# Layer norms whose sums over the partitions run on four 32-column groups and one folding product, with other products set between them

## Time and profile before

| | us |
|---|---|
| median of 3 runs (lowest, highest) | 2003.59 (2003.43, 2006.44) |
| the profiled execution, its own time | 2002.64 |
| its span, first to last instruction | 2000.9 |
| TensorE busy | 1972.6 (99%) |
| VectorE, ScalarE busy | 752.6 (38%), 401.2 (20%) |
| weights and inputs moved | 510.86 MB, 255 GB/s in the mean |

### The profile page before, as it was taken

How to read it: one execution, slowest core, us unless ns; L and a number is a source line. 1 busy time by engine, 2 the same in 40 slices (tenths; PEclk the granted TensorE clock), 3 DMA queues, 4 the chain that set the end, 5 groups by cost and what they waited for, 6 DMA issues and landing times.

```text
span 2000.9 us, 36477 instructions
## 1 busy us (share of the span) xinstructions
PE 1972.6 (99%) x15686; PEld 1437.2 (72%) x15686; DVE 752.6 (38%) x1766; ACT 401.2 (20%) x945; POOL 0.2 (0%) x4
## 2 busy tenths in 40 slices
PE   9999999999999999999999999999999999999998
PEld 8879999988766656666666666556764578566797
DVE  6847556587521111111111111011317734426725
ACT  1242110114310111000100010000214342223343
POOL 0000000000000000000000000000000000000000
PEclk9999999999999999999999999999999999999999
DMA  9474644455199999999999999999231211122220
GB/s 351 167 279 154 210 169 185 148 210 190 65 416 420 420 420 420 420 420 420 420 420 420 421 421 417 420 420 421 121 105 43 106 43 64 63 103 87 106 85 22
DMA packets 74929, 510.86 MB, mean 255 GB/s; under 512 B 7888, under 2 KB 13200, under 8 KB 13968
## 3 DMA queue, kind: packets, MB, share of 16 engines
q1 hardware_dynamic: 74768, 508.51, 63.6%
HBM read 507.40 MB, written 1.08 MB: 254 GB/s over the span
## 4 chain that ended last, share of the span: by engine, by line
PE 93%; DMA 4%; DVE 1%; ACT 1%; issue 0%; SPq 0%; DVEq 0%; ACTq 0%
PE ps L477 91%; DMA ring<-weights 3%; DMA work<-weights 1%; PE ps L1249 1%; PE ps L798 1%; PE ps L669 0%; DVE spare L2701 0%; DVE work L2092 0%; ACT work L1578 0%; PE ps L1409 0%; DVE small L2876 0%; ACT work L1889 0%; DVE work L2873 0%; SPq L1515 0%; PE ps L1363 0%
## 5 line engine op out<-in xcount | busy, mean ns | idle before, releaser
L477 PE MATMUL ps<-work 128*32 128x256 f32 (+8 forms) x4912 | 515.6, 375 | 3.5 <-DVE work L2396 0.9
L477 PE MATMUL ps<-work,ring 128*128 128x256 f32 (+2 forms) x1992 | 502.1, 406 | 1.0 <-DVE work L2841 1.0
L477 PEld LDWEIGHTS ps<-work 128*32 128x32 f32 (+3 forms) x4912 | 344.9, 142 | 134.3 <-issue 68.7
L477 PEld LDWEIGHTS ps<-work,ring 128*128 128x128 f32 x1992 | 339.3, 190 | 134.5 <-issue 106.9
L477 PE MATMUL ps<-ring,work 128*32 128x256 f32 (+3 forms) x4392 | 405.8, 407 | 3.0 <-DMA ring<-weights 2.4
L477 PEld LDWEIGHTS ps<-ring,work 128*32 128x32 f32 (+1 forms) x4392 | 234.4, 120 | 129.3 <-issue 59.3
L477 PE MATMUL ps<-xc,ring 128*128 128x256 f32 (+1 forms) x1344 | 252.9, 348 | 0.6 <-DVE xc L2097 0.6
L477 PEld LDWEIGHTS ps<-xc,ring 128*128 128x128 f32 x1344 | 222.5, 191 | 32.0 <-issue 5.3
L2354 DVE TENSOR_TENSOR work<-work,ps 128x256 f32<-128x256 f32 x42 | 17.7, 421 | 411.7 <-ACT work L1722 411.7
L1722 ACT ACTIVATE work<-ps 128x256 f32<-128x256 f32 x42 | 16.1, 384 | 556.6 <-PE ps L477 556.6
L477 PE MATMUL ps<-spare,work 128*32 128x256 f32 (+1 forms) x1128 | 120.4, 427 | 2.5 <-DMA ring<-weights 1.3
(11 more groups left out here) (283 smaller groups left out, 1248.9 us busy)
## 6 DMA issues: line engine op xcount, KB each, us to landing
ring<-weights SPq DMA_DIRECT2D x287, 1024.0 KB, 14.5
work<-weights SPq DMA_DIRECT2D x130, 1024.0 KB, 19.7
spare<-weights SPq DMA_DIRECT2D x54, 1024.0 KB, 19.5
work<-rel SPq DMA_DIRECT2D x8, 512.0 KB, 13.1
spare<-rows SPq DMA_DIRECT2D x2, 2048.0 KB, 9.5
con<-consts SPq DMA_DIRECT2D x1, 1368.0 KB, 22.2
work<-x_t SPq DMA_DIRECT2D x1, 1024.0 KB, 5.0
xc<-ctx_t SPq DMA_DIRECT2D x1, 1024.0 KB, 26.4
```

The source lines that it names most:

```text
L477: ins = eng.matmul(o, lhs, rhs, start=start, stop=stop, **kw)
```

## The change

Eight of the sums are made in another way: the means of `in`, `ln2_0` and `ln2_1`, and the variances of `ln1_0`, `ln2_0`, `ln1_1`, `ln2_1` and `rms0`. Chunk `c` is multiplied with 32 columns of ones into the 32 rows `32*(c % 4)` of the bank, so that four chunks go to four column groups of the array and each group adds up two chunks. ScalarE copies the bank, times 1/32, into `sums4`, and one product of `ones` with `sums4` folds the four partial sums into the full one. The variance is taken in two halves of four chunks. Between the halves, and between sums and fold, other products are set: embedding products at `ln1`, context products at `ln2_1` and `rms0`, turns and the second condition row at `ln2_0`, three spins at `in`. The semaphore `norm_std` becomes `norm_sums`, which counts copies and roots. In ScalarE's order at the context, the squares of `rms0` move ahead of context copies 1 to 4. No transfer is added or taken away.

```diff
 OUTS = [n for n in NORMS if not n.startswith("conv")]
+FOLDED_MEAN = ["in", "ln2_0", "ln2_1"]
+FOLDED_VAR = ["ln1_0", "ln2_0", "ln1_1", "ln2_1", "rms0"]
...
+        steps = [(kind, n) for n in NORMS for kind, those in (("mean", FOLDED_MEAN), ("var", FOLDED_VAR), ("std", NORMS))
+                 if n in those]
+        SUMS = {step: i + 1 for i, step in enumerate(steps)}
         def chunks_of(name):
...
+            def group_sum(o, c, v):
+                q = COL * (c % 4)
+                return mm(o[q:q + COL, 0:T], ones[:, 0:COL], v, c < 4, c >= 4)
+            def mean_parts(name, src):
+                o = fill(("mean_parts", name), 0, (s["norm_sums"], SUMS["mean", name]))
+                for c in range(KC):
+                    if normk(name) > 1:
+                        eng.wait_ge(*source(name, c))
+                    last = group_sum(o, c, src[:, c, 0:T])
+                last.then_inc(bank_full[0], 1)
+            def var_parts(name, centred):
+                o = fill(("var_parts", name), 1, (s["norm_sums"], SUMS["var", name]))
+                for c in range(KC):
+                    eng.wait_ge(s["norm_squared"], before(name) + c + 1)
+                    last = group_sum(o, c, squares(name, centred)[:, c, 0:T])
+                    if c == 3:
+                        yield
+                last.then_inc(bank_full[1], 1)
+                yield
+            def fold_parts(kind, name):
+                b, read_by = (1, (s["norm_sums"], SUMS["std", name])) if kind == "var" else \
+                    (0, (s["norm_centered"], before(name) + KC))
+                o = fill((kind, name), b, read_by)
+                mm(o[:, 0:T], ones, sums4, True, True).then_inc(bank_full[b], 1)
+            def advance(work, n):
+                for _ in range(n):
+                    next(work, None)
             def norm_mean_summed(l):
...
                 condition_rows(1, -2, 7)
-                norm_mean("ln2_0", res, KC, T)
+                mean_parts("ln2_0", res)
                 mod_t = fill(("mod_early",), 5, (s["mod_out"], 2))
                 condition_turns(1, -2, mod_t)
-                norm_var("ln2_0", KC, T, True)
+                fold_parts("mean", "ln2_0")
                 condition_rows(1, -1, 4)
+                var = var_parts("ln2_0", True)
+                next(var), next(var)
+                fold_parts("var", "ln2_0")
                 condition_turns(1, -1, mod_t).then_inc(bank_full[5], 1)
...
-            def router_beside_embedding():
-                products = ple_products(1)
-                for _ in range(KC):
-                    next(products)
+            def norm_beside_embedding(l):
+                products, var = ple_products(l), var_parts(f"ln1_{l}", True)
+                advance(products, 5)
+                next(var)
+                advance(products, 2)
+                next(var)
+                advance(products, 2)
+                fold_parts("var", f"ln1_{l}")
+                return products
+            def router_beside_embedding(products):
+                advance(products, 3)
                 o = fill(("logits",), 0, (s["logits_out"], 1))
...
                         last.then_inc(bank_full[0], 1)
-                    next(products)
+                    if c < 4:
+                        next(products)
                 assert next(products, "ended") == "ended"
...
                     o = fill(("ctx", c), 2 + c, (s["ctx_copied"], c + 1))
-                    first_tile(0, units[-1], c, o, T, 1).then_inc(bank_full[2 + c], 1)
-                norm_mean("ln2_1", res, KC, T)
+                    for k in range(KC):
+                        at = k * GW + (c % 2) * P
+                        last = mm(o[:, 0:T], units[-1][:, at:at + P], xn[:, k, 1, :], k == 0, k == KC - 1)
+                        if k == KC - 1:
+                            last.then_inc(bank_full[2 + c], 1)
+                        yield
+                mean_parts("ln2_1", res)
                 eng.wait_ge(s["norm_out_a"], KC)
-                context_tile(0)
-                norm_var("ln2_1", KC, T, True)
-                context_tile(1)
-                context_tile(2)
-                norm_var("rms0", KC, T, False)
-                context_tile(3)
-                context_tile(4)
+                context = chain.from_iterable(context_tile(c) for c in range(CC + 1))
+                advance(context, 2)
+                fold_parts("mean", "ln2_1")
+                for name, centred, n in (("ln2_1", True, (5, 2, 2)), ("rms0", False, (11, 6, 2))):
+                    var = var_parts(name, centred)
+                    for k in range(2):
+                        advance(context, n[k])
+                        next(var)
+                    advance(context, n[2])
+                    fold_parts("var", name)
+                for _ in context:
+                    pass
                 units.append(next_unit(beside=True))
...
             eng.wait_ge(s["x_loaded"], 16)
-            norm_mean("in", res, KC, T)
+            mean_parts("in", res)
+            spin(3)
+            fold_parts("mean", "in")
             spin(3)
...
                 norm_mean_summed(l)
-                norm_var(f"ln1_{l}", KC, T, True)
+                products = norm_beside_embedding(l)
                 if l == 0:
-                    for _ in ple_products(l):
+                    for _ in products:
                         pass
...
                 else:
-                    router_beside_embedding()
+                    router_beside_embedding(products)
                     turn_tokens()
...
                 load_root_table()
+                if name in FOLDED_MEAN:
+                    parts_copy("mean", name)
                 to, a = squares(name, centred), cen if centred else src
...
+            def parts_copy(kind, name):
+                o = tile(eng, kind + "_parts", name)
+                eng.activation(sums4, o[:, 0:T], ACT.Copy, scale=1.0 / COL).then_inc(s["norm_sums"], 1)
             def norm_std(name, chunks, n, centred=True):
+                if name in FOLDED_VAR:
+                    parts_copy("var", name)
                 o, eps = (rstd1, "eps5") if centred else (rstd2, "eps6")
                 v = tile(eng, "var", name)
-                inverse_root(o[:, 0:n], v[:, 0:n], eps, chunks * P).then_inc(s["norm_std"], 1)
+                inverse_root(o[:, 0:n], v[:, 0:n], eps, chunks * P).then_inc(s["norm_sums"], 1)
...
                 norm_std("ln2_1", KC, T)
+                norm_squares("rms0", KC, T, centred=False, src=xc)
                 copy(1)
-                norm_squares("rms0", KC, T, centred=False, src=xc)
+                norm_std("rms0", KC, T, centred=False)
                 copy(2)
-                norm_std("rms0", KC, T, centred=False)
                 copy(3)
...
```

More of the change, by code:

```diff
@@ L1 @@
 from contextlib import ExitStack
-from itertools import cycle
+from itertools import chain, cycle
 import numpy as np
@@ L248, in build @@
         cond_row = cut(2, T)
-        std1, rstd1, sig_sb = cut(T), cut(T), cut(2, T)
+        sums4, rstd1, sig_sb = cut(T), cut(T), cut(2, T)
         cond_s = cut(KC, 32)
@@ L331, in build @@
         names = """weights_used consts_loaded x_loaded params_loaded late_loaded rel_loaded rel_ready out_stored
-            norm_src res_summed sq_summed norm_centered norm_squared norm_std norm_scaled norm_out norm_out_a coef_out
+            norm_src res_summed sq_summed norm_centered norm_squared norm_sums norm_scaled norm_out norm_out_a coef_out
             cond_ready cond_row prep_done glu_gate glu_out qk_out v_out mod_out xo_half x_half conv_mixed
@@ L510, in norm_var_summed @@
             def norm_var_summed(name, summed):
-                o = fill(("var", name), 1, (s["norm_std"], normk(name)))
+                o = fill(("var", name), 1, (s["norm_sums"], SUMS["std", name]))
                 eng.wait_ge(s["sq_summed"], summed)
@@ L518, in norm_var @@
             def norm_var(name, chunks, n, centred, bank=0):
-                k, base = normk(name), before(name)
-                o = fill(("var", name), bank + 1, (s["norm_std"], k))
+                base = before(name)
+                o = fill(("var", name), bank + 1, (s["norm_sums"], SUMS["std", name]))
                 b = squares(name, centred)
@@ L2073, in norm @@
                     beside()
-                eng.wait_ge(s["norm_std"], k)
+                eng.wait_ge(s["norm_sums"], SUMS["std", name])
                 to = cen if centred else (xn if dst is None else dst)
@@ L2088, in final_norm @@
             def final_norm():
-                eng.wait_ge(s["norm_std"], normk("final"))
+                eng.wait_ge(s["norm_sums"], SUMS["std", "final"])
                 for c in range(KC):
```

## The result

The changed kernel takes **1993.59 us** (median of five runs, 1992.73 to 1994.45) against 2003.53 (2003.08 to 2006.44) on the same chip: ratio 0.9949, interval 0.9939 to 0.9960. Forecast were 1992.3, in a range of 1989 to 1999. In a second series it took 1993.81 against 2003.30 (0.9952, 0.9939 to 0.9966). The profiled execution took 1994.45 (span 1992.4), the upper end of its runs, where that of the kernel before was at the lower end of its own; so the two traces lie 8.5 us apart and the medians 9.9.

A forecast was written before the change was run, and what follows sets the result against it. TensorE, busy 99% of the span, was taken to bound the kernel, with norm chains where it lacks other work. Gains of 1.26+1.7+0.95+1.9+5.5=11.3 us gave 1992.3 us; 8-in-10 range 1989 to 1999.

The forecast's parts named there:

- ln2_0: Norm before the second projection: fold without cover, root 0.94 us earlier, TensorE's advance shrinks to the root's; gain 0.95 us.
- a root of `ln1_0`: At `ln1_0` the root starts 0.86 us later, since products stand ahead of the sums.
- VectorE late at the dense layer: After `ln1_0`, the dense layer's fifth product waits for VectorE's weight sums; only 1.7 of 3.0 us is kept.
- The chains take it back: Rival, 18%: at `ln1_0`, `ln2_0`, `ln1_1` the later root eats what TensorE saves; 1996.8 us.
- The experts don't move: Rival, 8%: the experts' end is not tied to the routing, so only the last place counts; 1998.1 us.
- don't run beside each other: Rival, 5%: the four column groups don't run in parallel, each sum costs 3.45 us again; 2010.7 us.
- a clock below 1.00 around 400: Sign of being wrong: TensorE's granted clock falls below the 2.4 GHz level around 400 us, near `ln2_0`.
- a longer expert stage: Sign of being wrong: the expert stage takes longer than before.
- The way back from tiles: Return from 32-column tiled products to whole products on TensorE: priced at 0.09 us, the same as the way in.
- half a group of four: Four tiled products, half a variance, between whole products: priced at 0.66 us of TensorE.
- in: First norm: mean by tiled sums and fold, centring at 8.69 instead of 9.95 us; gain 1.26 us up to the projection.
- The experts: Expert stage, from the router's end to the mean of `ln2_1`: moves as a block with the routing, its own term 0.

The follow-up runs named there:

- no_context: Changed kernel with the context place (`ln2_1`, `rms0`) left as in the kernel before; 1998.30 us, ratio 0.9976 to the kernel before.
- context_only: Kernel before with only the context place changed (mean of `ln2_1`, variances of `ln2_1` and `rms0`, ScalarE's order there); 1998.47 us, ratio 0.9975.
- unsplit_hold: Changed kernel with each variance in one go instead of two halves, plus eight throwaway products around the variance of `ln2_0`; 1991.82 us.
- unsplit_seventeen: Changed kernel with variances in one go, plus 17 throwaway products: eight at `ln2_0`, nine behind the places of the routing; 1994.77 us.
- spin_route: Changed kernel plus five throwaway 128-column products between token transposes and expert counts; 1993.56 us, ratio 0.9953 to the kernel before.
- unsplit: Changed kernel with each variance in one go instead of two halves; 1992.21 us, ratio 0.9939 to the kernel before.
- spin_both: Changed kernel plus five throwaway products ahead of the expert counts and eight around the variance of `ln2_0`; 1996.28 us, ratio 0.9963.
- after: The changed kernel itself, with all eight sums folded, against the kernel before; 1993.59 us, ratio 0.9949.

## Why the prediction was right, and where its terms were off

The mechanism was right at every place but `ln2_0`, where the clock came in: rounds of four 0.22 apart, a root of `ln1_0` that comes later against the mean (by 1.03, not 0.86), VectorE late at the dense layer (1.01 us of idle TensorE in two pieces, not 1.4), the counts behind VectorE's choice, a gain at both sides of the experts. "The chains take it back" (1996.8) and "The experts don't move" fell by `no_context`, "don't run beside each other" by the timelines. Two of the four signs that the prediction had named for being wrong did show, a clock below 1.00 around 400 and a longer expert stage; what they cost together was too little to leave its range. The sum was 11.3 and the two profiles give 8.5 and 9.8. The terms that were mis-sized:

- **The way back from tiles: 0.09 predicted, 0.19 measured.** The row that shows it was there: the record at 104.59 lasts 0.48 and not 0.38. I took the later start of that record from the row and not its length, so "half a group of four" cost 0.77 and not 0.66, and eight at one go 1.10. The context has five such returns before the gates: 5x0.104=0.52, and 22.9+0.52=23.4 is what was measured (23.46). The `ln1` norms have two ahead of the root, 0.2 of the 0.3 and all of the 0.2 that are missing there. The Trainium skill ("TensorEngine Tiling (Array Packing)", Tiling Modes, Key Properties) says that a change of tiling drains the engine. The prediction held 0.09 against that and estimated a whole drain at 0.16. The measured trip of 0.33 is nearer to two such drains (0.32) than to twice 0.09, though it is not split evenly (0.09 in, 0.19 out, some 0.05 in the staggered starts of a round); a sum with the rule would have been 1.3 us smaller, 10.0, beside the 9.9 of the medians.
- **`in`: 1.26 predicted, 0.86 in the first profile.** The step was sized with the clock up from 6.06 on, as in the trace before; in this execution it rose at 6.78, and the tiled records began at 6.47 and not 6.30. In the second profile it rose at 5.92 and the term was 1.21. Over the twelve profiles of kernels with this edit the term goes with that moment (3.97: 1.81; 4.96: 1.68; 5.46: 1.44; 5.92: 1.21; 6.35: 1.01; 6.78: 0.86; 7.09: 0.70, and the five others between), and `context_only`, without the edit, is 0.46 *late* with a rise at 7.00. With a rise at 6.08, nearest to the trace's own 6.06, it is 1.14 (`unsplit_hold`), and around 7.00 the kernels with and without the edit lie some 1.2 apart: the size was right within about 0.1, the rest is the execution's.
- **`ln2_0`: 0.95 predicted, 0.48 and 0.64.** Here a sentence of the prediction was wrong: that the clock is no rival of weight, as the stretch from 395.5 to 400.7 was no barer than that around the routing. The clock fell behind it in five of the six profiles that have the new `ln2_0` without throwaway products, in none of the six with them there and in neither of the two with the old one. In the five it fell 392.53 us after the first rise, wherever between 4.96 and 6.82 that stood; the sixth, `no_context`, had the earliest rise, 3.97, so the same work keeps the clock or loses it with the execution. Without a fall the term is 0.95 to 1.11. The row that I rested on the earlier trace rows was one execution's: `context_only` has the same work there and fell.
- **The experts: 0 predicted, 0.85 and 0.11 given back.** From the router's end to the mean of `ln2_1` every profile here is 0.1 to 1.8 us longer than that of the kernel before (`unsplit_seventeen` 2.0, of which 1.98 is its wait at the mean), and `context_only`, where nothing ahead of it is changed, by 0.89. So a longer stage does not need the change; in part it is the one execution that all are measured against, 0.95 below its own median. The fall behind the routing is not the reason in general, as `spin_route`, without it, has 0.71. A longer fall may add to it, which is not shown: of the eleven runs of `context_only` the two with the lowest mean clock (0.997; the profiled one fell there for 6.83 us) are the two slowest, 1999.24 and 1999.74. What makes the stage longer in one execution than in another stays open.

By medians the change is worth 9.9 against 11.3: the way back (0.9 over `ln1_0`, `ln1_1` and the context) and the clock behind `ln2_0` (0.3 to 0.5) are most of the 1.4.

## What to carry to other kernels

Sums on 32-column groups side by side pay even with a copy and a fold behind them, but every return to whole products costs, 0.34 us a round trip here: put tiled work in one piece, and fill the copy's time with whole products. Price a switch by the start and the length of the first record behind it, and take a granted clock of 1.00 in one profiled execution for what that execution had, not for a property of the stretch. Where TensorE is kept at work with throwaway products, use as few as do it: they move the place at which TensorE waits for its code, here a few us behind a branch, and that place may lie in a hot stretch.

## What the hardware showed that was not expected

- The change back to whole products takes 0.19 us in two pieces (0.09 before the first record, 0.10 before the second), the change into tiles 0.09.
- A wait of 1.17 to 1.22 us for nothing that the profile names stands once among the experts of every kernel here (between 558 and 571); its cause is open. A second one is seen within a mean if the place falls there: 0.39 to 1.98 us, ending 5.5 to 5.9 us behind a branch, moved by throwaway products that stand as far as 1000 us ahead of it.
- The clock fell to the 1.2 GHz level behind `ln2_0` with no wait over 0.84 us ahead of it in the timeline; in `unsplit` it fell at 535.89, behind router products of eight columns, with no idle stretch over 0.09 us in the 13 us before; and over the routing's 1.44 us it did not.
- The 3.41 us at half clock behind `ln2_0` cost 0.2 to 0.8 us (0.27 to 0.75 gained with them, 0.95 to 1.11 without), as VectorE sets the pace of its first part; those in the context of `spin_both` cost 1.7; those behind the routing nothing that the medians of `after` and `spin_route` show (1993.59 and 1993.56).
